# A two-layer hybrid decoder step on eight cores: other DMA constants in the planner that sets the instruction order

## The reference, cut to what matters

```python
for l in range(DEPTH):                       # DEPTH = 2
    q, k, v, u = _project(hp, ln1[l], w_in[l])          # rmsnorm, (.., 1024) @ (1024, 1280)
    q = _rope(q, pos_p); k = _rope(k, pos_p)
    a  = _prompt_attention(q, k, v, attn_sinks[l])      # 8 heads, 2 kv heads, window 128, learned sinks
    pm = _pool_mix(u, pos_p, L, pool_w[l], pool_scale[l])  # causal means over 2/4/8/16 rows
    hp = hp + jnp.einsum('bte,ed->btd', jnp.concatenate([a, pm], axis=-1), w_out[l])
    hp = hp + _mlp(hp, ln2[l], w_up[l], w_down[l])      # relu(x @ (1024, 4096))**2 @ (4096, 1024)
```

## Time and profile before

| | |
|---|---|
| median of 3 runs | 3265.5 us |
| the three runs | 2894.59, 3265.5, 3342.91 us |
| the profiled execution | 2896.64 us |
| its span on the slowest core (core 5) | 2895.1 us |
| spans of the eight cores | 2836.9 to 2895.1 us |
| TensorE busy | 2722.9 us (94%), 15774 matmuls |
| VectorE, ScalarE busy | 59%, 52% |
| mean granted TensorE clock, core 5 | 0.981 |

### The profile page before, as it was taken

The page is one execution under the profiler, slowest core; times in us unless marked ns, Lnnn a source line. Parts: engine busy times, 40 slices in busy tenths (PEclk is TensorE's granted clock), DMA queues, the critical chain, the costliest instruction groups (busy, mean ns, idle before and its releaser), DMA issues.

```text
span 2895.1 us, 50018 instructions; the slowest of 8 cores (2836.9 to 2895.1 us)
## 1 busy us (share of the span) xinstructions
PE 2722.9 (94%) x15774; PEld 1377.1 (48%) x15774; DVE 1715.8 (59%) x3839; ACT 1517.7 (52%) x3770; POOL 197.6 (7%) x336
## 2 busy tenths in 40 slices
PE   3778998999999999999899999999999999999997
PEld 1444444445454544545354555444454545444444
DVE  3555635656465665657365657566665666566654
ACT  2545535555354544556354556555655556555543
POOL 1000000100000000010000000000000000000000
PEclk8889999999999999999999999999999999999999
DMA  9679896762668557385945343353425242342446
GB/s 179 93 114 175 139 215 147 182 187 92 205 140 198 129 137 184 103 225 141 245 119 171 124 172 104 126 164 106 163 88 189 88 177 100 125 153 88 163 147 232
DMA packets 120761, 436.27 MB, mean 151 GB/s; under 512 B 18732, under 2 KB 49420, under 8 KB 86360
## 3 DMA queue, kind: packets, MB, share of 16 engines
q0 software_dynamic: 94144, 335.80, 45.4%
q1 hardware_dynamic: 26360, 97.28, 10.0%
HBM read 450.71 MB, written 79.22 MB: 183 GB/s over the span
## 4 chain that ended last, share of the span: by engine, by line
PE 78%; DMA 16%; issue 2%; ACT 2%; DVE 2%; SPq 0%; POOL 0%; ACTq 0%; DVEq 0%; POOLq 0%
PE ps_all L1148 27%; PE ps_all L1130 26%; PE ps_all L797 9%; PE ps_all L1069 8%; DMA h_mid<-s_h 4%; DMA s_h<-x_p 3%; DMA s_h<-h_mid 3%; PE ps_all L999 2%; PE ps_all L588 2%; DMA s_wout<-w_out 2%; DMA s_wup<-w_up 1%; DMA s_wdn<-w_dn 1%; PE ps_all L1013 1%; PE ps_all L949 1%; PE ps_all L950 1%
## 5 line engine op out<-in xcount | busy, mean ns | idle before, releaser
L1152 DVE TENSOR_TENSOR s_h<-s_h,ps_all 128x512 f32<-128x512 f32 x1072 | 732.4, 686 | 540.8 <-PE ps_all L1148 527.2
L1148 PE MATMUL ps_all<-s_wdn,s_aT 128*128 128x512 bf16 x4288 | 1036.0, 381 | 16.5 <-DMA s_wdn<-dn_bf 8.4
L1130 PE MATMUL ps_all<-s_xn2T,s_wup 128*128 128x512 bf16 (+2 forms) x4608 | 1015.6, 367 | 24.6 <-DMA s_wup<-w_up 14.3
L1130 PEld LDWEIGHTS ps_all<-s_xn2T,s_wup 128*128 128x128 bf16 x4608 | 448.8, 98 | 504.9 <-issue 43.5
L1148 PEld LDWEIGHTS ps_all<-s_wdn,s_aT 128*128 128x128 bf16 x4288 | 407.4, 98 | 466.7 <-issue 45.7
L1134 ACT ACTIVATE s_relu<-ps_all 128x512 f32<-128x512 f32 (+2 forms) x576 | 326.4, 567 | 549.0 <-PE ps_all L1130 537.1
L1135 ACT ACTIVATE s_aT<-s_relu 128x512 bf16<-128x512 f32 (+2 forms) x576 | 345.3, 600 | 57.3 <-PE ps_all L1148 27.6
L797 PE MATMUL ps_all<-s_win,s_xnT 128*128 128x512 bf16 (+1 forms) x1632 | 322.7, 351 | 36.0 <-DMA s_win<-w_in 12.7
L576 ACT ACTIVATE s_xhat<-s_h 128x1024 bf16<-128x1024 f32 x135 | 142.4, 1055 | 322.9 <-DVE s_stat L961 101.1
L974 ACT ACTIVATE s_P<-ps_all,s_stat 128x256 bf16<-128x256 f32 x520 | 239.1, 473 | 97.4 <-DVE s_stat L964 95.1
L1069 PE MATMUL ps_all<-s_wout,s_mixT 128*128 128x512 bf16 x1072 | 251.9, 384 | 1.8 <-DVE s_wout L748 0.9
(11 more groups left out here) (125 smaller groups left out, 1803.5 us busy)
## 6 DMA issues: line engine op xcount, KB each, us to landing
s_wup<-up_bf POOLq DMA_DIRECT2D x124, 1024.0 KB, 6.0
s_wdn<-dn_bf POOLq DMA_DIRECT2D x124, 1024.0 KB, 6.2
s_wup<-w_up POOLq DMA_DIRECT2D x20, 1024.0 KB, 15.7
s_wdn<-w_dn POOLq DMA_DIRECT2D x20, 1024.0 KB, 13.0
h_mid<-s_h SPq DMA_DIRECT2D x34, 512.0 KB, 8.6
s_h<-h_mid SPq DMA_DIRECT2D x34, 512.0 KB, 8.8
s_h<-x_p SPq DMA_DIRECT2D x32, 512.0 KB, 9.6
y_p<-s_h SPq DMA_DIRECT2D x32, 512.0 KB, 7.4
```

Of the source, the lines that this page charges most:

```text
L1130: r = e.matmul(ps_t[bk][:, 0:n], lhsT=wup_t[s][:, k, fc * 128:(fc + 1) * 128], rhs=x2[:, k, 0:n], start=(k == 0), stop=(k == 7))
L1148: r = e.matmul(ps_t[db][:], lhsT=aT[:, fc, j * 128:(j + 1) * 128], rhs=wdn_t[s][:, fc, hf * 512:(hf + 1) * 512], start=(fc == 0), stop=(fc ...
L1152: dve(lambda e, hf=hf, db=db: e.tensor_tensor(out=h_t[hs][:, hf * 512:(hf + 1) * 512], in0=h_t[hs][:, hf * 512:(hf + 1) * 512], in1=ps_t[d ...
```

## The change: three constants of the planner

The assumed rate of GpSimd's queue falls from 330,000 to 260,000 bytes per us, that of SyncE's and ScalarE's queues from 200,000 to 150,000, and the latency behind a transfer, 2.0 us for all before, becomes 3.0 us on GpSimd's queue and 5.0 us on the other two. No operation, tile, buffer or dependency changes; only the order on each engine does. Line numbers of the change are one higher than before.

```diff
--- before.py
+++ after.py
@@ -90,7 +90,8 @@
     return od.eng == "pe" and o.eng == "pe" and not od.dma and not o.dma
 
 ENGS = ("pe", "act", "dve", "pool", "sp")
-DMA_BW = {"pool": 330e3, "sp": 200e3, "act": 200e3}
+DMA_BW = {"pool": 260e3, "sp": 150e3, "act": 150e3}
+DMA_LAT = {"pool": 3.0, "sp": 5.0, "act": 5.0}
 HOP_LAT = 0.35
 SELF_LAT = 0.06
 
@@ -128,7 +129,7 @@
         if o.dma:
             issue_end = st + c
             dma_free[e] = max(issue_end, dma_free[e]) + nb / DMA_BW[e]
-            fin = dma_free[e] + 2.0
+            fin = dma_free[e] + DMA_LAT[e]
             eng_free[e] = issue_end
         else:
             fin = st + c
```

## The result

| | before | the change |
|---|---|---|
| median of four runs beside each other | 3082.6 us | 2848.66 us |
| ratio, from comparable runs | | 0.9831, 95% interval 0.9802 to 0.9859 |
| the profiled execution | 2896.64 us | 2850.05 us |
| slowest and fastest core in it | 2895.1, 2836.9 us | 2848.5, 2834.8 us |

The median of before is high because two of its four runs (3265.5 and 3342.91 us) were disturbed, as one of the change's was, 3199.28 us at a granted clock of 0.86 on one die; the ratio and all that follows leave such runs out. The change wins 46.6 us in the profiled executions where 25.9 were forecast: 2850 us in place of 2870. The range held the result; the size was wrong by 20 us.

A forecast was written before the change was run, and what follows sets the result against it. TensorE, busy 2722.9 of 2895.1 us, was taken to lose time waiting on late tile transfers at group boundaries. 21 + 6.6 + 9 + 2 - 2 + 0 - 15.7 + 5 = 25.9 us off 2896.64 gave 2870 us, range 2840 to 2898.

The forecast's parts named there:

- item 4: Float32 weights, 230 to 470 us: 15 us of waits go, 13 return; 2 us charged for later boundaries' weight loads.
- Item 5: Boundary at 577 us: first tile load now also behind cache copies, a wait of 4 to 6 us stays, nothing won.
- item 6: End of attention in three groups: cover for the last tile's norm and copies runs out, 15.7 us lost.
- item 1: Regular boundaries, 790 to 1700 us: waits for late tile loads fall from 27.2 to 6 us, 21 us won.
- Item 2: Boundaries of layer 1: first tile's transposes move by 7 to 9 us, waits go, 6.6 us won.
- item 7: The tail: more work between release and use of the last group's `up` weights, 5 us won.
- place 3: New `s_wdn1` load near 414 us loses cover: 13.8 us of matmuls against a 22.2 us landing, 8.4 us wait.
- Item 3: Granted clock: drops after boundary waits go, 8 us from 790 to 1700 us and 1 in layer 1, 9 won.
- Rival A: More is won: each wait removed brings its neighbours on time, 64 us, 2833 us (2820 to 2848); chance 0.17.
- B: Time only moved: boundaries of layer 0 give 24 us back to weight loads, 2894 us (2885 to 2905); chance 0.17.
- C: Slower: end of attention bounds every boundary, 2914 or 2957 us (2910 and above); chance 0.08 together with D.
- D: Transfers land as early as the planner thought, so waits have another cause: 2907 us; chance 0.08 together with C.

The follow-up runs named there:

- e10: The kernel before, unchanged, profiled a second time: ratio 1.0018 to its other executions, cores between 2864.8 and 2892.1 us.
- e5: Old constants for what the plan starts before 175 us, the change's new ones after: 2878.9 us, ratio 0.9882 to the kernel before.
- e9: The kernel before, order unchanged, with tile transfers of 128 KB in place of 512: 2854.25 us, ratio 0.9799.
- e0: The change again with no edit: 2853.25 us, ratio 0.9798 to the kernel before.
- e6: The change with the cache copies moved, 1 MB at a time, into groups 1 to 4 of layer 1: 2845.9 us, ratio 0.9778.
- e7: The change with residual tiles of groups 3, 10 and 12 planned at 250,000 bytes per us and 2 us latency: 2835.19 us, ratio 0.9746.
- e8: The change with both the moved cache copies and the three replanned groups: 2830.53 us, ratio 0.9731.
- e3: The change's new constants for what the plan starts before 175 us, the old ones after: 2887.95 and 2888.0 us.
- e4: The kernel before with only group 0's piece 5 `up` matmuls moved behind the transposes and pooling matmuls beside them: one execution, 2897.3 us.
- e11: The same single move of group 0's piece 5 `up` matmuls in the kernel before, measured again: 2898.53 us, ratio 0.9983.
- e1: The kernel before with only GpSimd's queue on the new constants: 2876.51 us, ratio 0.9863.
- e2: The kernel before with only SyncE's and ScalarE's queues on the new constants: 2882.2 us, ratio 0.9899.

## Why the prediction was wrong, by its own steps

Core 5 before and after, cut at the first `up` matmul of an MLP, against the prediction's items put into the same stretches:

| stretch | forecast | measured |
|---|---|---|
| start to group 1 (priced at zero) | 0 | -21.7 us |
| groups 1 to 4 (items 4 and 5, item 6 at group 3) | +4.9 | -4.0 |
| groups 5 to 9 (item 1 with its clock, conversions, item 6 on the way to group 10) | -24.2 | -21.9 |
| group 10 to the end (items 2 and 7, item 6 at group 12) | -6.6 | -8.1 |
| sum | -25.9 | -55.7 |

The slowest core of the change is another one, hence 46.6 and not 55.7. The table holds for core 5, the slowest of before, where the boundary waits were longest. On the mean of six cores of the same two profiles the stretches give -19.6, +4.5, -1.3 and -1.5 us, and with e10 as the kernel before -20.3, -3.6, -9.2 and -5.8. Only the start is the same in all three.

**The failed step is the sentence "The first 230 us hold the largest idle time, but the order there hardly changes".** The start was worth 20 us in the pair of profiles that was forecast: 237.7 -> 218.1 us to group 1 in the mean. Over all profiles it is 18: group 1 begins at 237.7, 238.4, 239.7 (e5) and 241.4 us (e9) with the old order there, and at 218.1, 220.0 (e0), 221.2 (e6, e7), 221.3 (e8) and 224.2 us (e3) with the new one. At the end of the program e3 stands 20 to 24 us under before. Nor does the order there hardly change: TensorE's first 1035 matmuls, up to group 1, differ in some 20 places. One of them moves the first `up` matmuls of piece 5 from 11.8 to 17.5 us behind the release of their buffer, in the one place of the start where a float32 load of 20.6 us was left bare by so much. The prediction used that very subtraction, landing time less work laid in between, for place 3, and not here, where the row stood in the trace: 8.8 us with the clock's drop behind it. e4 and e11 give that piece 10 to 12 of the 18 us by group 1, but only 7 of the mean at the end. For the rest, 6 to 8 us by group 1 and 12 to 17 at the end, no single move was tried, so its place stays open; the changed kernel also starts group 0's MLP 5 us earlier. e1 has most of the start's gain (223.5 us to group 1) and e2 next to nothing (237.3), so it hangs on the constants of GpSimd's queue.

**Item 1 was right on the core that it priced.** The 27.2 us of the earlier trace rows went but for 4.7 us at `s_xhat`, of which 3.8 are the end of attention at 1671 us (item 6), and e9 shows the cause that it named. Its stretch gave 22 us where 24 stood; the mean over the cores gained only 1 to 9 us there: other cores had less to lose (core 1 of before is busy 902.43 of the same 910 us), and all of them lost at group 10. The forecast for the whole, with the start taken out, is tested by e5. Its slowest core won 31 to 34 us where 25.9 were forecast, and its time was 2870.32 us at its fastest and 2878.9 in the median, where the forecast was 2870: near, and partly by the luck of a favourable profile as its base.

**Item 2 was right** (no boundary wait is left from 1850 to 2720 us), **and item 7 nearly** (8.4 us of waits became 1.5, priced at 5; the last group's MLP is 7 us shorter in the mean). From 2760 us on TensorE of the changed kernel waits only for

```profile
PE ps_all L1149 <- DMA s_wdn<-dn_bf: 1.5, 2, 1.1
```

**Item 3 was right in the regular stretch** (1.00 for 0.99); the larger part of what the clock gave lay again in the start, 0.91 -> 0.96 from 100 to 235 us, 0.05 x 135 = 7 us at most.

**Item 4 was right in its costs and a little low in the sum.** The predicted wait for `s_wdn1` came, 5.96 us where 8.4 was worked out, as the load took 18.9 us and not the 22.21; the waits for `s_wup` came to 6.5 us where the earlier trace rows had 5.6. All waits from 230 to 470 us fell from 25.3 to 12.5 us. As time it is less: groups 1 and 2 together take 349.4 us in the mean where they took 346.9, with item 6's loss at group 3 inside; in e7, where most of that loss is taken back, they take 342.5. So item 4 won some 4 us, where 2 stood.

**Item 5 named the wrong wait.** No wait for a tile's load of 4 to 6 us is left at 577 us, although the copies still stand ahead of it. The copies' cost appeared at the next boundary, at 758 us, in loads of another queue: 7.8 us with the second wait, 10 with the clock (e6). Item 4 had charged 2 us for the weight loads of all later boundaries together. Waits from 470 to 790 us rose from 8.1 to 16.6 us, of which 5.7 are item 6. The prediction quoted the Trainium skill, "DMA: Bandwidth & Descriptors", section "Issuing engines are not separate DMA queues", that transfers of all issuing engines meet on the same 16 DMA engines. This run agrees: with the copies gone from SyncE's queue the weight load on GpSimd's is on time. It was used to doubt items 1 and 2, whose waits went all the same, instead of asking which load would run beside the 2 MB now.

**Item 6 was right in its places and too low in the sum.** 4.26 + 1.47 us at 568.72, 3.18 + 0.59 + 1.03 at 1671, 3.46 + 1.47 and 2.31 near 2000 are 17.8 us of waits, against 12.7 and 3 for the clock. As time the loss is 3 to 6 us over groups 2 and 3, 9 to 11 over 9 and 10, and 7 over 11 and 12 (all waits of these groups together), some 20 us where 15.7 stood; the way to group 10, priced at 2.8 us, is what was most too low. e7, which restores part of the cover, won 17 us of the mean.

**Rival A** said that item 4 pays in full, item 6 costs nothing and the start gives 6 us. Its time (2820 to 2848) nearly came true, but not for its reasons as a whole: the start gave three times its 6 us and the tail about its sum, item 4 did not pay in full, and item 6 cost more than was said. **B** and **C** fell: between 790 and 1700 us the weight waits are 2.8 us in all, and only the three groups of item 6 wait by more than 1 us at the end of attention; what B described happened at one boundary, at 758 us. **D** fell with e9.

A part of the change's effect on the metric is seen only over all cores: it makes them alike. The spread falls from 48 to 21 us over all executions, and since the slowest core is the time, the time falls by more than the mean, 56 against 43 us; the 13 us between them are a quarter of it. e2 and e5 close the spread (21 and 25 us), e1 and e3 do not (49 and 50), so it hangs on the later order and SyncE's constants.

## What to carry to other kernels

Where an order changes, subtract for every load the work between its buffer's release and its first use from the landing time the trace shows, in all of the program and first where loads are longest; "the order hardly changes" is no price when one row in it uncovers or covers a load of 20 us. The constants of a planner are a means to an order: one set for all moved the regular boundaries into the clear and took the cover from three others, and other constants for those three were worth another half per cent. They were not nearer to the truth: e7 plans a tile there at 4.1 us, where the medians of the changed kernel are 7.2 to 12.9. So try them by stage, and judge each by the waits and by the time of its stage. With eight independent cores compare the spans of all of them over several executions before trusting one profile of the slowest.

## What the runs showed of the hardware

- Tile transfers of 512 KB took 8.6, 8.8 and 9.6 us in the median (stores to h_mid, loads from it, loads of x_p), those of 128 KB at the same places of the same order 5.0, 6.7 and 5.4: with three quarters of the bytes gone, over half of the time stays.
- A 2 MB copy from DRAM to DRAM on SyncE's queue delayed 1 MB weight loads on GpSimd's; with the copies elsewhere (e6) the loads of the same 50 us took 6.3 to 10.3 us. The three loads of `s_wup` issued from 722.7 to 750.3 us in the changed kernel, then the median of all 124 of it:

```profile
DMA to landing us min/median/max: 6.6/18.3/21.4
```

```profile
s_wup<-up_bf POOLq DMA_DIRECT2D x124, 1024.0 KB, 5.4
```

- The same program differed on one core by 54 us between two profiled executions (core 7 before: 2837.9 and 2892.1 us): 12 us up to group 1, 16 in groups 1 to 4, 17 in groups 5 to 8 and 9 after. With the landing times of tiles covered by work (the change) or short (e9) the cores of one execution differ by 21 and 25 us, where they differed by 48.
